# Two-layer block kernel: the order in which two mixers load projection chunks and modulation slots

## Chip, cores and metric

One core of one Trainium2 chip (trn2). The metric is the device time of one execution in microseconds, the median of three runs. Everything is float32 in memory.

## What is computed

The reference runs two blocks of two layers each over 256 tokens of width 1024. Only the first block's mixers matter here. Cut to that:

```python
cond = silu(c)
for layer in range(2):
    mod = dot(cond, ada_w[layer]) + ada_b[layer]          # 1024 -> 6144
    sh1, sc1, g1, sh2, sc2, g2 = split(mod, 6)
    u = x * (1 + sc1) + sh1
    proj = u @ w_in[layer]                                # 1024 -> 3088: six chunks of 512 and 16 "low" columns
    ...                                                   # short convolution, gated linear attention, w_out
    x = layernorm(ALPHA * x + (1 + g1) * mix)
    u = x * (1 + sc2) + sh2
    ...                                                   # feed-forward
```

The first third of the modulation (sh1, sc1) is wanted before u can be formed. The other two thirds are wanted only after the mixer, so the kernel computes them between the pieces of the input projection.

## The kernel before

The program is a list of stages (`stages()`), which every engine walks in the same order; the engines meet only at semaphores. The stage touched is "gla", which occurs twice, once per layer of the first block (the first and the second mixer). It starts with a stretch that computes `proj` and the other two thirds of `mod`:

- **Chunks.** C0 to C5 are each 1024 x 512 of `w_in`, 2 MiB. Matmuls are made from rounded halves: ACT rounds a quarter of a chunk into `l_hi` (`linear` in the scalar block, L1409 to L1426), DVE takes the remainder into `l_lo` (`linear_rest`, L1835), and TensorE multiplies hi by hi, hi by lo and lo by hi (`linear` in the tensor block, L741), 48 matmuls of 512 columns in each chunk. `l_hi` and `l_lo` have two buffers each, so a quarter is split while the one before it is multiplied. A filled chunk is copied by DVE into `proj` (L2160).
- **Slots.** A0 to A7 are each 256 x 2048 of `ada_w`, 2 MiB. `ada_slot` (L1068) multiplies one with `cond`, 16 small matmuls. It waits for both halves of its load. Slots A0 to A3 make modulation group 1, A4 to A7 group 2. When a group is complete ACT gathers it into `ada_rows` (`gather_rows`, L1428), TensorE spreads the rows over all partitions (`ada_spread_rows`, L1079) and DVE adds the bias (`add_rows`, L1842).
- **Low.** The last 16 columns of `w_in`, a load of 64 KB, multiplied after all chunks and slots (L1134). Everything of the gated attention follows it.

All 15 loads go through the two buffers `wide[0]` and `wide[1]` in turn: load w lies in buffer w % 2 (`RW = 2`). SP issues them in a fixed order, each as two halves of 1 MiB, and waits before each half until the buffer is free again (`fill`, L507 to L521, `wait_slot`, L498). A buffer that held a chunk is free for a first half when the remainder of its second quarter has been taken, and for the second half after the fourth; a buffer that held a slot is free for both when TensorE has used the slot. SP waits in order: a load that can't be issued holds up all behind it.

The order is written out by hand in three constants at the head of the file. `GLA_CHUNK_AT[c]` is the place of chunk c among the 15 loads, `GLA_ADA_AT[c]` are the places of the slots that TensorE uses behind chunk c, and low is at place 14:

```python
GLA_CHUNK_AT = (0, 2, 4, 7, 9, 11)
GLA_ADA_AT = ((1,), (3,), (5, 6), (8,), (10,), (12, 13))
```

So the order before is C0 A0 C1 A1 C2 A2 A3 C3 A4 C4 A5 C5 A6 A7 low. Group 1 is complete behind C2; its rows are spread in two parts, behind C3 and C4 (`ada_between`), and added by DVE one chunk later (`add_between`). ACT gathers group 1 after the second quarter of C3 (L1616).

Of the kernel before, what the change touches and what calls it, by code (L numbers as in the profile page):

```python
# [75 lines left out]

ADA_SLOTS = 4
ADA_COLS = 2048
GLA_CHUNK_AT = (0, 2, 4, 7, 9, 11)
GLA_ADA_AT = ((1,), (3,), (5, 6), (8,), (10,), (12, 13))  # L80
GLA_LOW_AT = 14


# [106 lines left out]
def build(nc, I, out):  # L190
# [29 lines left out]
    with ExitStack() as ctx:  # L220
# [8 lines left out]
        A = ctx.enter_context(nc.psum_tensor("A", [P, 4, 512], F32))  # L229
# [414 lines left out]
        def _(pe):  # L644
# [434 lines left out]
            def ada_spread_rows(group, banks, js=range(4)):  # L1079

                pe.wait_ge(ada_rows_ready, group + 1)
                for j in js:
                    if len(banks) == 4:
                        pe.wait_ge(ada_read, 4 * group)
                    elif group or j >= 2:
                        pe.wait_ge(ada_read, 4 * group + j - 1)
                    mm(banks[j % len(banks)], ones[32 * j:32 * j + 1, :], ada_rows[32 * j:32 * j + 1, :], True, True) \
                        .then_inc(ada_spread, 1)

            second_half = None  # L1090
            for index, (kind, arg, n, before) in enumerate(steps):
# [26 lines left out]
                elif kind == "gla":  # L1118
                    pe.wait_ge(t_evac, n.tg)

                    def ada_between(c):

                        for i, at in enumerate(GLA_ADA_AT[c]):
                            s = sum(map(len, GLA_ADA_AT[:c])) + i
                            group = 3 * arg + 1 + s // ADA_SLOTS
                            if s == 0 and n.free:
                                pe.wait_ge(acc_free, n.free)
                            ada_slot(n.w + at, group, s % ADA_SLOTS, A[:, 2 + s // ADA_SLOTS, :])
                        if c in (3, 4):
                            ada_spread_rows(3 * arg + 1, (A[:, 0, :], A[:, 1, :]), range(2 * c - 6, 2 * c - 4))  # L1130

                    linear(n, 6, uhv, ulv, 2, open_banks(n), linear_bank, g_done, True, between=ada_between)

# [232 lines left out]
        def _(act):  # L1366
# [222 lines left out]
            for index, (kind, arg, n, before) in enumerate(steps):  # L1589
                if kind == "start":  # L1590
                    act.wait_ge(s_c, 16)
                    nc.scalar.activation(condT, cT, ACT.Silu).then_inc(cond_ready, 1)
                elif kind == "ada":
                    gather_rows(3 * arg, G[:, 0, :])
                elif kind in ("trs8", "trs16"):
                    next_kind, m = split_early(index)
                    if next_kind == "ffn":
                        for q in range(4):
                            dense_rounder(m)(0, 0, q)
                    elif next_kind:  # L1600
                        linear(m, range(2))
                    groups = 4 if kind == "trs16" else 2
                    dst = (yh if kind == "trs16" else uh)[:, :].rearrange("p (k s) -> p k s", k=4 * groups)
                    for i in range(T * groups):
                        t, j = divmod(i, groups)
                        act.wait_ge(t_done, n.tg + i + 1)
                        nc.scalar.activation(dst[:, 4 * j:4 * j + 4, t * P:(t + 1) * P],
                                             TB[:, (n.tg + i) % 2, :].rearrange("p (k s) -> p k s", k=4), ACT.Copy) \
                            .then_inc(act_ready, 1)
                elif kind in ("out1", "out2"):  # L1610
                    linear(n, range(2, 8 if kind == "out1" else 16), acc_done, lambda c: n.acc + c + 1)
                elif kind == "tr8":
                    for j in range(4):
                        evac(n.tg + j, uT[:, 2 * j:2 * j + 2, :])
                elif kind == "gla":
                    linear(n, range(2, 14), g_done, lambda c: n.g + 2 * c + 2, slots=GLA_CHUNK_AT)  # L1616
                    gather_rows(3 * arg + 1, A[:, 2, :])
                    linear(n, range(14, 24), g_done, lambda c: n.g + 2 * c + 2, slots=GLA_CHUNK_AT)
                    gather_rows(3 * arg + 2, A[:, 3, :])
                    evac(n.tg, glowT[0:RANK, :], S, RANK)  # L1620
                    for t in range(T):
                        log_gate(n.g + 12 + t, lsg[:, t, :], KW)

                    evac(n.tg + 1, small[:, 52:60], 8, P, ACT.Exp)
                    act.wait_ge(dve_ready, n.dve + 3)
                    for t in range(T):
                        g = n.g + 16 + t
                        act.wait_ge(g_done, g + 1)
                        nc.scalar.activation(e3[:, t, 0:2 * KW], G[:, g % 2, 0:2 * KW], ACT.Exp)
                        nc.scalar.activation(e3[:, t, 2 * KW:3 * KW], G[:, g % 2, 0:KW], ACT.Exp, scale=-1.0) \  # L1630
                            .then_inc(act_ready, 1)
                    evac(n.tg + 2, gqT)
                    evac(n.tg + 3, gkT)
                    for t in range(T):
                        act.wait_ge(g_read, n.g + 16)
                        nc.scalar.activation(proj[:, t, C_H:C_H + VW], proj[:, t, C_G:C_G + VW], ACT.Silu) \
                            .then_inc(act_ready, 1)
                    for t in range(T):
                        g = n.g + 20 + t
                        act.wait_ge(g_done, g + 1)  # L1640
                        for h in range(HEADS):
                            sum_squares(g, t, h, DV, hbuf[:, t * VW + h * DV:t * VW + (h + 1) * DV], h == HEADS - 1)
                elif kind == "ffn":
                    run_dense(n)
                elif kind == "moe":
                    act.wait_ge(dve_ready, n.dve)
                    full = act.value_load(crowded[0:1, 0:1], min_val=0, max_val=1)
                    with act.If(full == 0):
                        with act.Fori(0, EXPERTS // 2) as i:
                            run_packed(n, i)  # L1650
                        act.drain().then_inc(act_ready, 3 * NU * EXPERTS - ACT_PAIR * (EXPERTS // 2))
                    with act.Else():
                        with act.Fori(0, EXPERTS // 2) as i:
                            run(n, PAIR, straight, i * PAIR, None)
                elif kind == "router":
                    act.wait_ge(dve_ready, n.dve + 1)
                    nc.scalar.activation(e2, gap, ACT.Exp).then_inc(act_ready, 1)
                elif kind == "kvdown":
                    for t in range(T):
                        act.wait_ge(g_done, n.g + t + 1)  # L1660
                        sum_squares(n.g + t, t, 0, KVLORA, sg[:, t * KVLORA:(t + 1) * KVLORA], True)
                    evac(n.tg, ckvT)
                    evac(n.tg + 1, krT, S)
                elif kind == "fox":
                    linear(n, range(2, 24), g_done, lambda c: n.g + 2 * c + 2)
                    for t in range(T):
                        log_gate(n.g + 12 + t, flt[:, t, :], FOX_H)
                    evac(n.tg, ncT[0:FOX_H, :], S, FOX_H, ACT.Copy, -1.0)
                    attention(n.tg + 1, 0)
                elif kind == "mla":  # L1670
                    for t in range(T):
                        act.wait_ge(g_done, n.g + t + 1)
                        sum_squares(n.g + t, t, 0, QLORA, hbuf[:, t * QLORA:(t + 1) * QLORA], True)
                    evac(n.tg, cqT[:, 0:2, :])
                    evac(n.tg + 1, cqT[:, 2, :], S)
                    for j in range(4):
                        evac(n.tg + 2 + j, qrT[:, 2 * j:2 * j + 2, :])
                    attention(n.tg + 6, GROUPS)
                elif kind == "ple":
                    linear(n, range(2, 8), g_done, lambda c: n.g + 2 * c + 2)  # L1680
                    evac(n.tg, pT)
                    for t in range(T):
                        act.wait_ge(g_read, n.g + 3 + t)
                        nc.scalar.activation(gt[:, t, :], gt[:, t, :], ACT.Sigmoid).then_inc(act_ready, 1)
# [73 lines left out]
        def _(dve):  # L1758
# [382 lines left out]
            for index, (kind, arg, n, before) in enumerate(steps):  # L2141
# [12 lines left out]
                elif kind == "gla":  # L2154

                    def add_between(c):
                        if c in (4, 5):
                            add_rows(arg, 1, (A[:, 0, :], A[:, 1, :]), range(2 * c - 8, 2 * c - 6))

                    linear(n, 6, lambda c, b: V.tensor_copy(proj[:, b, c * 512:(c + 1) * 512], linear_bank(c, b)),  # L2160
                           GLA_CHUNK_AT, add_between)
# [247 lines left out]
```

## Time and profile before

| | us |
|---|---|
| median of three runs | 2968.67 (2967.88 to 2969.22) |
| the profiled execution, its own time | 2973.35 |
| its span, first to last instruction | 2971.6 |
| first mixer: start of its C0, of its low projection | 57.15, 152.28 |
| second mixer: the same | 476.14, 572.55 |

The profile is of one execution. "PE" is TensorE's matmuls, "DVE" VectorE, "ACT" ScalarE, "SP" the engine whose queue issues the loads. Ends of matmuls are modelled, so durations of TensorE's work are best taken from start to start. Times are microseconds from the start of the span.

### The profile page before, as it was taken

The numbers are of one execution on the slowest core, as the hardware profiler recorded it, in microseconds if no ns is written. First come the engines' busy times: TensorE is split into PE (matmuls) and PEld (weight loads), VectorE is DVE, ScalarE is ACT, GpSimd is POOL, SyncE is SP. The second block draws the span as 40 slices with busy tenths as digits, with TensorE's granted clock in tenths as the row PEclk, the third lists the DMA queues.
The fourth block names the chain that finished last, engine by engine and source line by source line (L and its number), as shares of the span: only waits on it lengthen the run. The fifth ranks groups of instructions, "written<-read, shape, count | busy, mean of one in ns | idle before, by whom it ended". The sixth has DMA issues, their size and how long they took to land.

```text
span 2971.6 us, 33909 instructions
## 1 busy us (share of the span) xinstructions
PE 2598.4 (87%) x11836; PEld 2023.3 (68%) x11836; DVE 1714.6 (58%) x2044; ACT 1274.9 (43%) x1714; POOL 68.2 (2%) x88
## 2 busy tenths in 40 slices
PE   4978997767998998998999798988996998898996
PEld 2646874446776776776776686887874786687884
DVE  2446454455886886886787645535554554455545
ACT  1233432324665665665666333343431442043441
POOL 1000000000000000000000000000001000000001
PEclk7989998887999999999999899989998999999998
DMA  7816548724996996997899453406543643325551
GB/s 294 310 59 222 172 158 308 254 71 137 324 327 234 318 328 228 329 327 268 297 327 311 151 202 133 136 36 212 173 159 98 207 170 108 133 69 186 188 180 53
DMA packets 397402, 608.89 MB, mean 205 GB/s; under 512 B 14112, under 2 KB 317248, under 8 KB 390592
## 3 DMA queue, kind: packets, MB, share of 16 engines
q1 hardware_dynamic: 389648, 583.32, 57.3%
q0 software_dynamic: 6288, 22.55, 2.2%
q8 instruction: 87, 1.43, 0.2%
q10 hardware_dynamic: 1312, 1.05, 0.1%
q14 instruction: 67, 0.55, 0.1%
HBM read 605.83 MB, written 1.05 MB: 204 GB/s over the span
## 4 chain that ended last, share of the span: by engine, by line
PE 60%; DVE 17%; issue 12%; ACT 5%; DMA 4%; POOL 1%; ACTq 0%; DVEq 0%; SPq 0%
PE G L663 34%; PE A L663 18%; DVE w_lo L1876 9%; PE TB L663 4%; ACT w_hi L1463 4%; PE TB L685 2%; DMA wide<-in_moe_w_up 1%; PE TB L1036 1%; DVE hidden L1927 1%; DMA wide<-in_w_in 1%; DMA wide<-in_ada_w 1%; PE TB L935 1%; DVE small L2094 1%; DMA small<-in_c 1%; DVE x_tok L2106 1%
## 5 line engine op out<-in xcount | busy, mean ns | idle before, releaser
L1876 DVE TENSOR_TENSOR w_lo<-wide,w_hi 128x1024 fp32r<-128x1024 f32 x572 | 675.0, 1221 | 69.6 <-ACT w_hi L1463 65.3
L663 PE MATMUL G<-w_hi,u_hi 128*128 128x512 f32 x1584 | 646.6, 408 | 15.7 <-DVE u_lo L1901 6.4
L663 PE MATMUL G<-w_hi,u_lo 128*128 128x512 f32 x1584 | 621.9, 393 | 0.0
L663 PE MATMUL G<-w_lo,u_hi 128*128 128x512 f32 x1584 | 621.8, 393 | 0.0
L1463 ACT ACTIVATE w_hi<-wide 128x1024 fp32r<-128x1024 f32 x572 | 578.1, 1052 | 38.6 <-PE G L663 12.4
L663 PEld LDWEIGHTS G<-w_hi,u_hi 128*128 128x128 f32 x1584 | 299.8, 189 | 106.1 <-DVE w_lo L1876 34.9
L663 PEld LDWEIGHTS G<-w_hi,u_lo 128*128 128x128 f32 x1584 | 299.4, 189 | 66.0
L1876 DVE TENSOR_TENSOR w_lo<-down,w_hi 128x1024 fp32r<-128x1024 f32 x286 | 337.2, 1220 | 11.1 <-ACT w_hi L1463 10.4
L663 PEld LDWEIGHTS G<-w_lo,u_hi 128*128 128x128 f32 x1584 | 300.3, 190 | 57.9 <-issue 1.9
L663 PE MATMUL A<-w_hi,hidden_hi 128*128 128x512 f32 x792 | 317.3, 401 | 10.7 <-DVE w_lo L1876 10.7
L663 PE MATMUL A<-w_hi,hidden_lo 128*128 128x512 f32 x792 | 315.2, 398 | 0.0
L663 PE MATMUL A<-w_lo,hidden_hi 128*128 128x512 f32 x792 | 314.9, 398 | 0.0
L1838 DVE TENSOR_TENSOR l_lo<-wide,l_hi 128x1024 fp32r<-128x1024 f32 x128 | 155.9, 1224 | 237.3 <-ACT l_hi L1425 224.4
L1463 ACT ACTIVATE w_hi<-down 128x1024 fp32r<-128x1024 f32 x286 | 285.9, 1049 | 6.7 <-PE G L663 6.7
L1425 ACT ACTIVATE l_hi<-wide 128x1024 fp32r<-128x1024 f32 x128 | 134.3, 1059 | 294.7 <-PE G L663 101.7
L2001 DVE TENSOR_TENSOR hidden_lo<-TB,hidden_hi 128x512 fp32r<-128x512 f32 x50 | 34.6, 692 | 270.1 <-ACT hidden_hi L1551 270.1
L663 PEld LDWEIGHTS A<-w_hi,hidden_hi 128*128 128x128 f32 x792 | 149.7, 189 | 46.1 <-DVE w_lo L1876 11.7
L663 PEld LDWEIGHTS A<-w_hi,hidden_lo 128*128 128x128 f32 x792 | 150.2, 190 | 37.0
L663 PEld LDWEIGHTS A<-w_lo,hidden_hi 128*128 128x128 f32 x792 | 150.1, 190 | 35.6
L1551 ACT ACTIVATE hidden_hi<-TB 128x512 fp32r<-128x512 f32 x50 | 30.0, 600 | 261.1 <-PE TB L935 261.1
L1505 ACT ACTIVATE hidden_hi<-TB 128x256 fp32r<-128x256 f32 x88 | 33.9, 385 | 229.2 <-PE TB L1036 229.2
L1547 ACT ACTIVATE silu_gate<-G 128x256 f32<-128x256 f32 x110 | 42.5, 386 | 208.5 <-PE G L663 208.5
(252 smaller groups left out, 2919.1 us busy)
## 6 DMA issues: line engine op xcount, KB each, us to landing
wide<-in_moe_w_gate SPq DMA_DIRECT2D x88, 1024.0 KB, 5.5
wide<-in_moe_w_up SPq DMA_DIRECT2D x88, 1024.0 KB, 8.5
down<-in_moe_w_down SPq DMA_DIRECT2D x88, 1024.0 KB, 9.4
wide<-in_ffn_w_in SPq DMA_DIRECT2D x88, 1024.0 KB, 7.6
wide<-in_ada_w SPq DMA_DIRECT2D x48, 1024.0 KB, 7.1
down<-in_ffn_w_out SPq DMA_DIRECT2D x44, 1024.0 KB, 8.5
wide<-in_w_in SPq DMA_DIRECT2D x24, 1024.0 KB, 6.9
wide<-in_fox_w_in SPq DMA_DIRECT2D x12, 1024.0 KB, 5.2
```

Of the source, the lines that this page charges most:

```text
L663: return nc.tensor.matmul(o, lhsT, rhs, start=start, stop=stop, skip_group_check=True)
L685: last = nc.tensor.transpose(TB[:, tg % 2, b * P:(b + 1) * P], block_in, ident)
L935: last = nc.tensor.transpose(TB[:, (n.tg + j) % 2, f * S + t * P:f * S + (t + 1) * P], hid[:, 0, t, tok(f)], ident)
L1036: last = nc.tensor.transpose(TB[:, (n.tg + c) % 2, tok(f)], hid[:, 0, 0, tok(f)], ident)
L1425: nc.scalar.activation(ring[p % depth], wide[w % RW][:, q * 1024:(q + 1) * 1024], ACT.Copy) \
L1463: nc.scalar.activation(to[:, :], raw, ACT.Copy).then_inc(hi_ready, 1)
L1505: nc.scalar.activation(hth[:, 0:2 * P], TB[:, (n.tg + c) % 2, 0:2 * P], ACT.Copy).then_inc(act_ready, 1)
L1547: nc.scalar.activation(sgt[:, t, :], G[:, t, 0:FU], ACT.Silu).then_inc(act_ready, 1)
L1551: nc.scalar.activation(hth[:, :], TB[:, (n.tg + j) % 2, :], ACT.Copy).then_inc(act_ready, 1)
L1838: V.tensor_tensor(l_lo[at][:, :], wide[(n.w + slots[c]) % RW][:, q * 1024:(q + 1) * 1024], l_hi[at][:, :].bitcast(F32), ALU.subtract).then ...
L1876: V.tensor_tensor(w_lo[to][:, :], raw, w_hi[to][:, :].bitcast(F32), ALU.subtract).then_inc(lo_ready, 1)
L2001: V.tensor_tensor(htl[:, :], TB[:, (n.tg + j) % 2, :], hth[:, :].bitcast(F32), ALU.subtract) \
```

## The change

The three orders are rewritten: chunks go in pairs, then slots in pairs. The rows of group 1 are spread behind C4 and C5 in place of C3 and C4 and added by DVE one chunk later than before, and ACT gathers them after the second quarter of C4. The new order is C0 C1 A0 A1 C2 C3 A2 A3 C4 C5 A4 A5 A6 A7 low.

```diff
-GLA_CHUNK_AT = (0, 2, 4, 7, 9, 11)
-GLA_ADA_AT = ((1,), (3,), (5, 6), (8,), (10,), (12, 13))
+GLA_CHUNK_AT = (0, 1, 4, 5, 8, 9)
+GLA_ADA_AT = ((), (2, 3), (), (6, 7), (), (10, 11, 12, 13))
 GLA_LOW_AT = 14
...
-                        if c in (3, 4):
-                            ada_spread_rows(3 * arg + 1, (A[:, 0, :], A[:, 1, :]), range(2 * c - 6, 2 * c - 4))
+                        if c in (4, 5):
+                            ada_spread_rows(3 * arg + 1, (A[:, 0, :], A[:, 1, :]), range(2 * c - 8, 2 * c - 6))
...
-                    linear(n, range(2, 14), g_done, lambda c: n.g + 2 * c + 2, slots=GLA_CHUNK_AT)
+                    linear(n, range(2, 18), g_done, lambda c: n.g + 2 * c + 2, slots=GLA_CHUNK_AT)
                     gather_rows(3 * arg + 1, A[:, 2, :])
-                    linear(n, range(14, 24), g_done, lambda c: n.g + 2 * c + 2, slots=GLA_CHUNK_AT)
+                    linear(n, range(18, 24), g_done, lambda c: n.g + 2 * c + 2, slots=GLA_CHUNK_AT)
                     gather_rows(3 * arg + 2, A[:, 3, :])
...
-                        if c in (4, 5):
-                            add_rows(arg, 1, (A[:, 0, :], A[:, 1, :]), range(2 * c - 8, 2 * c - 6))
+                        if c in (5, 6):
+                            add_rows(arg, 1, (A[:, 0, :], A[:, 1, :]), range(2 * c - 10, 2 * c - 8))
```

## Rows read from the trace of the kernel before

**Rows 1.** The page, busy time, share of the span, instructions, by engine.

```profile
PE 2598.4 (87%) x11836; PEld 2023.3 (68%) x11836; DVE 1714.6 (58%) x2044; ACT 1274.9 (43%) x1714; POOL 68.2 (2%) x88
```

**Rows 2.** The page, the chain that ended last, shares by engine.

```profile
PE 60%; DVE 17%; issue 12%; ACT 5%; DMA 4%; POOL 1%; ACTq 0%; DVEq 0%; SPq 0%
```

**Rows 3.** TensorE's waits, 57 to 153 us: total, times, longest us.

```profile
PE TB L663 <- DVE l_lo L1838: 5.6, 1, 5.6
```

**Rows 4.** Timeline of TensorE, first mixer: start, us, instruction, idle before and releaser.

```profile
70.67 1.92 PE L663 MATMUL A<-wide,small 128*32 128x512 f32 x16
72.52 0.50 PE L663 MATMUL TB<-l_hi,u_hi 128*128 128x512 f32 x1
...
83.73 1.92 PE L663 MATMUL A<-wide,small 128*32 128x512 f32 x16
...
106.19 0.80 PE L663 MATMUL TB<-l_hi,u_hi 128*128 128x512 f32 x1 [5.60 <-DVE l_lo L1838]
...
119.14 1.92 PE L663 MATMUL A<-wide,small 128*32 128x512 f32 x16
...
122.05 0.50 PE L663 MATMUL G<-l_hi,u_hi 128*128 128x512 f32 x1
...
152.28 0.59 PE L663 MATMUL TB<-u_hi,wide 128*16 128x256 f32 x2 [1.14 <-DMA wide<-in_w_in]
```

**Rows 5.** Timeline of SP's queue, loads issued: start, us.

```profile
72.65 0.34 SPq L517 DMA_DIRECT2D wide<-in_ada_w  x1
73.03 0.43 SPq L519 DMA_DIRECT2D wide<-in_ada_w  x1
73.51 0.43 SPq L517 DMA_DIRECT2D wide<-in_w_in  x1
80.66 0.38 SPq L519 DMA_DIRECT2D wide<-in_w_in  x1
...
98.72 0.38 SPq L517 DMA_DIRECT2D wide<-in_w_in  x1
...
518.16 0.38 SPq L517 DMA_DIRECT2D wide<-in_w_in  x1
```

**Rows 6.** Landings: of 98.72; of 80.66; of 72.65 and 73.03; with 73.51.

```profile
DMA to landing us min/median/max: 5.1/5.1/5.1
...
DMA to landing us min/median/max: 5.2/5.2/5.2
...
DMA to landing us min/median/max: 5.0/6.1/7.2
...
DMA to landing us min/median/max: 5.0/7.2/9.3
```

**Rows 7.** Timeline of DVE, first mixer.

```profile
69.20 1.23 DVE L1838 TENSOR_TENSOR l_lo<-wide,l_hi 128x1024 fp32r<-128x1024 f32 x1 [1.57 <-ACT l_hi L1425]
...
104.91 2.36 DVE L1838 TENSOR_TENSOR l_lo<-wide,l_hi 128x1024 fp32r<-128x1024 f32 x2 [11.21 <-ACT l_hi L1425]
```

**Rows 8.** Stretches: length, busy us by engine, granted clock, DMA share, GB/s.

```profile
70.67:106.19 35.52, 29.92 (x161) 19.45 (x161) 12.17 (x13) 9.70 (x10) 0.00 (x0) 0.96 0.85 317
106.19:119.14 12.95, 12.95 (x48) 10.19 (x49) 5.96 (x6) 3.30 (x4) 0.00 (x0) 0.85 0.72 266
```

**Rows 9.** Timeline of TensorE, second mixer.

```profile
490.05 1.92 PE L663 MATMUL A<-wide,small 128*32 128x512 f32 x16
...
526.75 0.79 PE L663 MATMUL TB<-l_hi,u_hi 128*128 128x512 f32 x1 [6.65 <-DVE l_lo L1838]
...
539.33 1.92 PE L663 MATMUL A<-wide,small 128*32 128x512 f32 x16
...
572.55 0.59 PE L663 MATMUL TB<-u_hi,wide 128*16 128x256 f32 x2 [0.96 <-issue]
```

**Rows 10.** Timeline of DVE, behind the first mixer's low projection.

```profile
160.50 2.48 DVE L1848 TENSOR_TENSOR arena<-A,arena 128x512 f32<-128x512 f32 x4 [12.36 <-PE A L663]
```

**Rows 11.** Timeline of TensorE, the third slot ahead of the first mixer.

```profile
30.08 3.64 PE L663 MATMUL G<-wide,small 128*32 128x512 f32 x16 [6.56 <-DMA wide<-in_ada_w]
```

## The prediction

> **What bounds the kernel now.** I read the page first: busy times and the chain that ended last. TensorE is busy 87% of the span [rows 1], and 60% of the chain is TensorE with DMA at 4% [rows 2]. A load matters only where TensorE runs dry for it, so the question is where it does so inside the two mixers. The list of who waited for whom, taken over the first mixer's projection stretch (57.15 to 152.28 us), is led by 5.6 us put down to DVE's l_lo, the last link between a load and its product [rows 3]. The timeline of TensorE gives the places [rows 4]: 1.14 us ahead of the low projection at 152.28, and the 5.60 us ahead of the fourth chunk (C3), at 106.19, right behind the one place where two modulation slots follow each other. That chunk lay in a buffer freed only at the end of the first of the two slots: SP issued it at 98.72 [rows 5], its first half landed 5.1 us after the issue [rows 6], ACT rounded it, DVE took its remainder from 104.91 [rows 7], TensorE began at 106.19. So one rule governs: **a chunk behind a modulation slot in its own buffer comes 106.19 - 98.72 = 7.47 us after that slot is used.** Everywhere else one slot lies between chunk c and chunk c+1, the other buffer holds that slot, and the next chunk's halves load while chunk c is still multiplied. In that stretch DMA is 85% busy at 317 GB/s [rows 8]. The second mixer repeats it: 6.65 us ahead of C3 [rows 9].
>
> Unit prices, all start to start in rows 4: a chunk 83.73 - 72.52 = 11.21 us; a modulation slot 72.52 - 70.67 = 1.85; a slot with a spread of two rows behind it 122.05 - 119.14 = 2.91, the spread thus 1.06; the chunk behind the stall 119.14 - 106.19 = 12.95, so 1.74 more. In rows 9 the last is 539.33 - 526.75 = 12.58.
>
> **The change, step by step.** No instruction is added or removed: the same 6 chunks, 8 slots and 15 loads, hence the same bytes. What moves is the order, on TensorE, on SP (each load waits in order for its own buffer) and in two places on ACT and DVE. New order: C0 C1 A0 A1 C2 C3 A2 A3 C4 C5 A4 A5 A6 A7 low, even places in buffer 0, odd in buffer 1. I follow the first mixer from the end of C0, 70.67, which stays (C1 now loads in the place of A0, before C0 begins).
>
> 1. C1 follows C0 directly: 70.7 to 81.9. Its first weights must be split; in rows 7 the piece begun by DVE at 69.20 took 1.23 us and ended 70.43, so this is covered.
> 2. A0 runs to 83.7 (its buffer was free halfway through C0). A1's second half waits for C1's last split, which came 80.66 - 72.52 = 8.14 us into the chunk [rows 4, 5]: 78.8, plus 5.2 to land [rows 6] gives 84.0. A1 ends 85.9; 0.3 us lost.
> 3. C2 shares buffer 0 with A0. SP issues it at 83.75 and TensorE has it at 83.75 + 7.47 = 91.2. **Idle 5.3 us**, where before there was none. The chunk behind is the 12.95 us kind: to 104.2. C3, issued at 85.9 behind it, is in time: to 115.4.
> 4. The same again: A2 to 117.2, A3 to 119.4, C4 ready at 117.3 + 7.47 = 124.7. **Idle 5.3 us**, then 12.95 to 137.7. This stall stands for the old one at C3. Spread 1.06, C5 to 149.9.
> 5. The tail. Before, one slot stood before C5 and the last two were in or nearly so. Now four stand behind it, and two of them have no buffer until A4 and A5 are used. A4 ends 151.8. A5's second half is issued 138.7 + 8.14 = 146.9 and is in at 152.0; A5 ends 153.8. A6 is issued at 151.8: rows 6 give 5.0 us for the first half and 7.2 for the second issued 0.38 later, so it is in at 159.4. **Idle 5.6 us.** A7, issued 153.8, queues behind it; three halves in a row landed at 77.65, 80.2 and 82.8 [rows 5, 6], 2.6 us each, so A7 is in at 164.6. **Idle 3.3 us**, after A6 ended 161.3. A7 to 166.4, the spread that used to stand before C5 to 167.5. The low projection's small load, issued 161.3, lands before that, so its old 1.14 us wait is gone.
>
> Low starts at 167.5 instead of 152.28: **15.2 us later.** As a sum from 70.67: work is 5 x 11.21 + 8 x 1.85 + 2 x 1.06 = 73.0 both times; before 5.60 + 1.14 idle and 1.74 slow chunk make 81.5 (81.61 read); now about 20 idle and 3.5 slow. The added moves on the other engines are free: ACT's gather of the second group and two of DVE's adds (four took 2.48 us [rows 10], so 1.2 for the two, and the gather, of the same 512 columns, 0.6) now fall under the low projection, which with its spread filled 152.28 to 160.50, some 7 us without the spread. I cost them at nothing because that covers them; without it they would be 2 us per mixer. Nothing takes the delay up later: DVE had stood idle 12.36 us for TensorE before those adds [rows 10]. The loads of w_out behind are the next stage's.
>
> Second mixer, from 490.05 to 572.55 [rows 9], 82.5 us: the same list with 12.58 for 12.95 (twice) gives 96.1, so **13.6 us**. Here the issue at 518.16 took 8.59 us to the product instead of 7.47 [rows 5, 9]; the ends for each of the four boundary stalls are 7.47 and 8.59 and I keep 7.47, three of the neighbouring landings being 5.0 to 5.2.
>
> **TensorE's clock in the tail** is shown by no row. What the rows have: after an idle stretch of 6.56 us a modulation slot took 3.64 us instead of 1.92 [rows 11], and after 5.60 us a chunk lost 1.74. A6's loss hides in the wait for A7. For A7 and low I bound it by 0 (warm again) and 3.4 (two such losses), and take 1.0 per mixer, nearer to the lower end since A6 and A7 stand close together. On this the Trainium skill, "TensorE: Matmul & The Clock Gate", on oscillation, says that kernels with idle stretches for DMA between short bursts run their matmuls at half rate after every gap and pay half the throttled time. The trace agrees in kind: over the chunk behind the stall the granted clock was 0.85, against 0.96 over the stretch before it [rows 8]. And by that rule the tail's low projection could stay at 1.2 GHz; that is rival C.
>
> **Sum:** 15.2 + 13.6 + 2.0 = 30.8 us. The profiled execution has a span of 2971.6 and a time of 2973.35; with the change 3002.4 and 3004.15. The median of the runs is 2968.67, 4.7 below the profiled one, so I forecast **2999.5 us**. For the load latency, the skill's "DMA: Bandwidth & Descriptors", on the anatomy of one DMA, fits 2.0 us plus bytes over 436 GB/s, which is an estimated 4.4 us for a half of 1 MiB; rows 6 have 5.0 to 5.2, and the measurement decides. By that fit each of the six waits would be 0.6 to 0.8 shorter and the answer 2995.
>
> **Rivals.** (A) *Faster.* The pairing takes away the double slot between C2 and C3 and puts nothing in its place: the ring would cover C2 and C4 because the buffer opens early. Worth 5.60 + 1.74 + 6.65 + 1.4 = 15.4 us, 2953. It decides at one point: C2 must be issued by 85.9 - 7.47 = 78.4, over 5 us before A0 ends. Only if buffer 0 were given back before A0 was used could that be; SP's wait on the slot says no. (B) *No change.* The stage is bound by the rate of the loads (85% busy), the bytes are the same, and order doesn't matter: 2969. Against it: 28 MiB at 2.6 us per MiB are 73 us in 81.6, so there is slack for TensorE to set the pace, and the new order leaves DMA with nothing to do in C1's and C3's second halves. (C) *Clock.* The tail's gaps keep TensorE at 1.2 GHz through low, 7 us of work: 7 instead of 1 per mixer, 3011. For it: two gaps with only 1.85 us of work between them. Against: low is unbroken, and the chunk behind 5.60 us of idle lost only 1.74, so there the full rate came back within 4 us. (D) *Smaller.* The tail's wait is taken up elsewhere and only the boundaries count: (0.3 + 5.3 + 0.2 + 5.3 + 1.74 - 5.6) = 7.2 per mixer, 2983.
>
> **How the numbers follow.** Forecast, with its own bounds: 0.80. Rival C 0.08, D 0.04, A 0.04, B 0.04. Lower bound of the forecast: no loss in the tail (-2), and the chunks behind a stall at the plain 11.21 for the one new stall in each mixer (-3), and landings 0.6 shorter on six waits (-4): 2990. Upper: 8.59 on four boundary stalls (+4.5) and 3.4 instead of 1 in each tail (+5): 3009. That holds 8 in 10, so the range stays there. A measurement of this kernel can tell about 0.2% (6 us) from no change: faster 0.04, same 0.04, slower 0.92.
>
> **What would show it.** In the profile after: the waits of TensorE should have two stalls of 5 to 6 us per mixer, ahead of C2 and of C4, put down to DVE's l_lo, and none ahead of C3; two waits for DMA wide<-in_ada_w near the end, 5.6 and 3.3 us; SP issuing C2 right after A0 is used; low 15 us later than 152.28, the second mixer's low some 29 later than 572.55; everything between and behind shifted unchanged. The forecast is wrong if C2 begins within 2 us of A1's end, if A6 and A7 run back to back, or if the stretch between low and the next stage shrinks by what the tail grew.

## The result, and the profile after

The changed kernel takes 3001.21 us (median of 5 runs, 2999.35 to 3003.94) against 2969.22 us (5 runs) for the kernel before: a ratio of 1.0108, 95% interval 1.0094 to 1.0122, or 32.0 us more. Forecast was 2999.5. The profiled execution took 3002.36 us with a span of 3000.6, 29.0 us more than the span before.

The page answers to rows 1 and 2 almost without a change: TensorE is busy 7 us longer, with the same 11836 matmuls.

```profile
PE 2605.3 (87%) x11836; PEld 2025.7 (68%) x11836; DVE 1714.3 (57%) x2044; ACT 1274.0 (42%) x1714; POOL 68.1 (2%) x88
```

The waits of TensorE tell more. First mixer, 57 to 170 us, the view of rows 3:

```profile
PE G L663 <- DVE l_lo L1838: 13.7, 2, 7.2
PE A L663 <- DMA wide<-in_ada_w: 8.2, 3, 6.7
PE G L663 <- DVE u_lo L2057: 1.4, 1, 1.4
```

Second mixer, 480 to 610 us:

```profile
PE G L663 <- DVE l_lo L1838: 11.1, 2, 5.7
PE A L663 <- DMA wide<-in_ada_w: 7.1, 3, 5.7
```

Each mixer has two waits for a chunk in place of one, and 8.2 and 7.1 us of waits for slots, where the kernel before had none and 0.3. The timeline of TensorE, first mixer (as rows 4), has their places:

```profile
81.25 1.92 PE L663 MATMUL A<-wide,small 128*32 128x512 f32 x16
...
91.81 0.79 PE L663 MATMUL G<-l_hi,u_hi 128*128 128x512 f32 x1 [6.57 <-DVE l_lo L1838]
...
115.80 1.92 PE L663 MATMUL A<-wide,small 128*32 128x512 f32 x16
117.90 1.92 PE L663 MATMUL A<-wide,small 128*32 128x512 f32 x16 [0.18 <-DMA wide<-in_ada_w]
...
126.99 0.79 PE L663 MATMUL G<-l_hi,u_hi 128*128 128x512 f32 x1 [7.17 <-DVE l_lo L1838]
...
139.51 1.13 PE L663 MATMUL A<-ada_rows,con 1*128 1x512 f32 x4
...
162.31 3.64 PE L663 MATMUL A<-wide,small 128*32 128x512 f32 x16 [6.68 <-DMA wide<-in_ada_w]
...
167.25 3.64 PE L663 MATMUL A<-wide,small 128*32 128x512 f32 x16 [1.30 <-DMA wide<-in_ada_w]
...
171.89 0.61 PE L663 MATMUL TB<-u_hi,wide 128*16 128x256 f32 x2
...
178.90 1.14 PE L663 MATMUL A<-ada_rows,con 1*128 1x512 f32 x8
```

C2 at 91.81 and C4 at 126.99 are the two boundaries, A6 at 162.31 and A7 at 167.25 the tail, 171.89 the start of low, which has no wait of its own any more. The second mixer (as rows 9):

```profile
530.37 0.80 PE L663 MATMUL G<-l_hi,u_hi 128*128 128x512 f32 x1 [5.46 <-DVE l_lo L1838]
...
564.82 0.80 PE L663 MATMUL G<-l_hi,u_hi 128*128 128x512 f32 x1 [5.68 <-DVE l_lo L1838]
...
600.19 3.64 PE L663 MATMUL A<-wide,small 128*32 128x512 f32 x16 [5.65 <-DMA wide<-in_ada_w]
605.15 1.92 PE L663 MATMUL A<-wide,small 128*32 128x512 f32 x16 [1.32 <-DMA wide<-in_ada_w]
...
608.06 0.61 PE L663 MATMUL TB<-u_hi,wide 128*16 128x256 f32 x2
```

SP's queue shows when the chunks behind were issued (as rows 5): C2 right behind A0 (81.25 + 1.92), C4 behind A2.

```profile
83.23 0.38 SPq L517 DMA_DIRECT2D wide<-in_w_in  x1
...
117.78 0.38 SPq L517 DMA_DIRECT2D wide<-in_w_in  x1
...
522.99 0.38 SPq L517 DMA_DIRECT2D wide<-in_w_in  x1
...
557.10 0.38 SPq L517 DMA_DIRECT2D wide<-in_w_in  x1
```

From issue to product these are 8.58, 9.21, 7.38 and 7.72 us, where the kernel before had 7.47 and 8.59. Counted from C0 to the start of low, the stretch grew from 95.13 to 115.05 us in the first mixer (56.84 to 171.89) and from 96.41 to 111.89 in the second (496.17 to 608.06): 19.9 and 15.5 us, together 35.4. Behind the second mixer the offset between the two profiled executions shrank again to 29.0; the repeat of the kernel before, below, is about that.

### The profile page after: what moved, and what is told of

Read it like the earlier page. It is cut to its first block, busy times and chain, and to the rows that moved or that the text cites. A ratio compares the mean times of both kernels' runs of the same rounds, so it can differ in the third digit from the quotient of the medians.

```text
span 3000.6 us, 33909 instructions
## 1 busy us (share of the span) xinstructions
PE 2605.3 (87%) x11836; PEld 2025.7 (68%) x11836; DVE 1714.3 (57%) x2044; ACT 1274.0 (42%) x1714; POOL 68.1 (2%) x88
## 3 DMA queue, kind: packets, MB, share of 16 engines
q10 hardware_dynamic: 1312, 1.05, 0.1%
HBM read 605.83 MB, written 1.05 MB: 202 GB/s over the span
## 4 chain that ended last, share of the span: by engine, by line
PE 60%; DVE 18%; issue 12%; ACT 5%; DMA 4%; POOL 1%; ACTq 0%; DVEq 0%; SPq 0%
PE G L663 34%; PE A L663 17%; DVE w_lo L1876 10%; PE TB L663 4%; ACT w_hi L1463 4%; PE TB L685 2%; DMA wide<-in_ada_w 1%; PE TB L1036 1%; DVE hidden L1927 1%; DMA wide<-in_w_in 1%; PE TB L935 1%; DVE small L2094 1%; DMA small<-in_c 1%; DVE x_tok L2106 1%; DVE u_lo L2057 1%
## 5 line engine op out<-in xcount | busy, mean ns | idle before, releaser
L1876 DVE TENSOR_TENSOR w_lo<-down,w_hi 128x1024 fp32r<-128x1024 f32 x286 | 337.2, 1220 | 11.1 <-ACT w_hi L1463 10.5
```

Of the source, the lines that this page charges most:

```text
L1876: V.tensor_tensor(w_lo[to][:, :], raw, w_hi[to][:, :].bitcast(F32), ALU.subtract).then_inc(lo_ready, 1)
```

## Experiments

The theory is that of the forecast: a load can be issued only when TensorE has used the slot in its buffer, and is exposed wherever no more than one slot's work stands between; behind the wait some work runs at the lower clock. Four kernels were run first, two that split the change and two repeats.

**One pair alone.** The kernel before with C1 ahead of A0, and nothing else.

```diff
-GLA_CHUNK_AT = (0, 2, 4, 7, 9, 11)
-GLA_ADA_AT = ((1,), (3,), (5, 6), (8,), (10,), (12, 13))
+GLA_CHUNK_AT = (0, 1, 4, 7, 9, 11)
+GLA_ADA_AT = ((), (2, 3), (5, 6), (8,), (10,), (12, 13))
```

> The kernel before with one thing of the change: C1 comes ahead of A0, so that the order is C0 C1 A0 A1 C2 A2 A3 C3 and from there as before. Theory (a chunk that lies in the buffer of the slot just used comes about 7.5 us after that slot): a new stall of 5.3 to 6.6 us ahead of C2 in each mixer, the old one ahead of C3 stays, C2 loses 1.3 to 1.7 us to the half clock, tail unchanged: 7 to 8 us per mixer, 2983 to 2985 us in all, half of what the change cost. Rival (pairing chunks is free, all of the cost lies in the four slots at the end): 2969 us and no stall ahead of C2.

Measured: 2986.01 us, ratio 1.0058 (1.0041 to 1.0075), or 17.8 us more. Its waits of TensorE in the first mixer:

```profile
PE G L663 <- DVE l_lo L1838: 6.8, 1, 6.8
PE TB L663 <- DVE l_lo L1838: 5.8, 1, 5.8
```

The new one (G, an even chunk: C2) stands beside the old one (TB, an odd chunk: C3), in the second mixer as 5.8 beside 7.3. Pairing is not free; one boundary costs about 9 us per mixer. The interval of the ratio allows 6 to 11, so that this is more than the 7 to 8 expected is not shown. From issue to product the loads took 8.74 us (C2) and 7.69 (C3) in the first mixer, 7.64 and 9.29 in the second.

**The tail alone.** From the changed kernel, with a slot between all chunks up to C4:

```diff
-GLA_CHUNK_AT = (0, 1, 4, 5, 8, 9)
-GLA_ADA_AT = ((), (2, 3), (), (6, 7), (), (10, 11, 12, 13))
+GLA_CHUNK_AT = (0, 2, 4, 6, 8, 9)
+GLA_ADA_AT = ((1,), (3,), (5,), (7,), (), (10, 11, 12, 13))
```

> The other part alone: order C0 A0 C1 A1 C2 A2 C3 A3 C4 C5 A4 A5 A6 A7 low. Every chunk but C5 has a slot between it and the one before, so no stall ahead of C2, C3, C4; the four slots stand at the end as in the changed kernel. Theory: the old stall at C3 goes (minus 5.6 and 1.7 us; 6.65 and 1.4 in the second mixer), the tail costs two waits of 5.6 to 6.7 and 1.3 to 3.3 us plus slow slots, about 10 us per mixer against the tail before: plus 2 to 3 us per mixer, 2973 to 2975 us. Rival (the tail's waits are taken up behind the low projection, only the boundaries count): 7.5 us less per mixer, 2954 us. Rival (the clock stays at the lower level through low and beyond): 2985 us.

Measured: 2973.48 us (12 runs), ratio 1.0019 (1.0008 to 1.0030). The first mixer's waits before low:

```profile
PE A L663 <- DMA wide<-in_ada_w: 7.4, 3, 5.1
PE G L663 <- DVE u_lo L2057: 1.4, 1, 1.4
```

No wait for a chunk is left in the first mixer (the second keeps 0.70 us ahead of C3), and the slots' waits are there: 5.05 for A6, 1.71 for A7 and 0.62 for A5. The old stall gone and the tail added nearly cancel, as expected; both rivals (2954, 2985) are out. With the stall at 7.3 and 8.0 us per mixer this puts the two tails at 5.3 + 15.3 = 20.6 us. The changed kernel less one_pair, which has as many boundary stalls but the tail of before, gives 32.0 - 17.8 = 14.2. The profile's own count for the changed kernel (waits for A6 and A7 and what the slots took over 1.92, less the 1.14 and 0.96 that went ahead of low) is 18.0, between the two. The ratios' intervals are several us wide, so 14 to 21 us for the two tails is all that these three can say.

**The changed kernel again.**

> The changed kernel once more, for a second look at the four boundary waits and the two tail waits of each mixer. Theory: the longer ones of the first mixer (6.6, 7.2 and 6.7 us, where 5.3 to 5.6 were forecast) are late landings that vary from execution to execution; then they come out differently, between 5.3 and 7.2. Rival: something in the first mixer makes its loads slower each time; then the same three stand within 0.3 us, and the second mixer's at 5.5 to 5.7 again.

Measured: one run, 3005.05 us. From issue to product the four chunks took 8.77, 8.97, 7.91 and 7.35 us; the wait for A6 in the first mixer was 6.6 and in the second 5.6. This settles neither side. The three long waits of the first mixer came again as 6.7, 6.8 and 6.6 us, the second of them 0.4 off, outside the rival's 0.3; the second mixer's came as 6.1, 5.4 and 5.6. Long waits are not bound to the first mixer either: one_pair has its longest in the second, and so have both executions of the kernel before.

**The kernel before again.**

> The kernel before once more. In the two profiled executions the offset between the kernels fell from 35 us behind the second mixer to 29 us at the end, most of it in the expert stage. Theory: this is the spread of single executions in stages that the change doesn't touch; then this execution stands 2 to 6 us earlier than the first one at the end of the expert stage. Rival: the changed order shifts something that makes the expert stage shorter by 6 us; then this execution keeps within 1 us of the first one all the way.

Measured: one run, 2965.32 us. Matmul for matmul it stands 0.9 us behind the first execution at the start of the first mixer and 1.5 behind at the second mixer's low, then 3.4 ahead of it at 1630 us, 4.8 at 2237 and 8.0 at the end. This is one kernel against itself, so offsets of some us in the stages behind are the spread of single executions. Between the two repeats the offset does the opposite: 34.2 us at the second mixer's low, 39.7 at the end. So the 6 us that the first pair of executions seemed to give back are not shown to be an effect of the change. The two mixers themselves, from C0 to low, repeat more closely: 191.5 and 191.6 us in the kernel before, 226.9 and 224.0 in the changed one.

**Idle matmuls in the waits.** In `ada_between` of the changed kernel, behind each slot:

```diff
+                            if s in (1, 3):
+                                for _ in range(22):
+                                    mm(A[:, 0, :], uhv[:, 0, tok(0)], uh[:, 0:512], True, True)
+                            if s in (5, 6):
+                                pe.wait_ge(g_read, n.g + 10)
+                                for _ in range(22 if s == 5 else 10):
+                                    mm(G[:, 0, :], uhv[:, 0, tok(0)], uh[:, 0:512], True, True)
```

> The changed kernel with idle matmuls in its waits: 22 of 512 columns behind A1 and A3 (into a bank not yet in use), 22 behind A5 and 10 behind A6, in each mixer; the results are overwritten and nothing else is changed. They take 5.0 us and 2.3 us, less than the waits. Theory: the waits for loads stay, but TensorE goes on at 2.4 GHz behind them: C2 and C4 take 11.2 us instead of 12.5 to 12.9, A6 1.9 instead of 3.6 (partly given back as a longer wait for A7), A7 1.9 in both mixers: 3 to 5 us less per mixer, 2992 to 2995 us. Rival (the chunk behind a stall is slower because its splits come late, not through the clock): no change, 3001 us.

Measured: 2991.48 us, ratio to before 1.0072 (1.0059 to 1.0084), so about 10 us under the changed kernel with 152 more matmuls, just better than the expected range. The timeline of its first mixer behind C3:

```profile
113.22 1.92 PE L663 MATMUL A<-wide,small 128*32 128x512 f32 x16
116.38 1.92 PE L663 MATMUL A<-wide,small 128*32 128x512 f32 x16 [1.23 <-DMA wide<-in_ada_w]
```

C2, first product at 91.08, and C3 together took 22.14 us up to 113.22, where the changed kernel needed 115.80 - 91.81 = 23.99 and two undisturbed chunks are 22.42 by rows 4. C4 of the second mixer shows it best, first in the changed kernel, then here (as rows 8; the granted clock is third from the end):

```profile
564.82:578.55 13.73, 13.73 (x48) 10.75 (x48) 5.95 (x6) 3.29 (x4) 0.00 (x0) 0.80 0.70 253
...
554.19:565.40 11.21, 11.21 (x49) 8.86 (x49) 5.95 (x6) 3.30 (x4) 0.00 (x0) 1.00 0.87 318
```

All four chunks behind a wait took 11.1 to 11.2 us at the full clock, against 12.5 to 13.7 at 0.79 to 0.88, and A6 and A7 took 1.92 each. The first halves still landed 5.1 to 6.3 us after their issue and no split got shorter, so the slower chunk is the clock's. Not all of the 10 us is: the four landings add up to 21.8 us here and to 23.3 and 23.5 in the two executions of the changed kernel. The clock's part there is thus an estimated 8 us or a little more (the kernel before has some of it too, at its C3).

**One slot between any two chunks.** From the changed kernel:

```diff
-GLA_CHUNK_AT = (0, 1, 4, 5, 8, 9)
-GLA_ADA_AT = ((), (2, 3), (), (6, 7), (), (10, 11, 12, 13))
+GLA_CHUNK_AT = (0, 2, 4, 6, 8, 10)
+GLA_ADA_AT = ((1,), (3,), (5,), (7,), (9,), (11, 12, 13))
```

> Order C0 A0 C1 A1 C2 A2 C3 A3 C4 A4 C5 A5 A6 A7 low: one slot between any two chunks, three at the end. Theory: no stall ahead of any chunk, and one wait in the tail, for A7, which gets its buffer only when A5 has been used: 5.6 us plus 0 to 1.7 for its clock; the 1.1 us ahead of low go. Against before minus 7.3 and plus 5 to 6 per mixer: 2965 to 2968 us, within 0.2 per cent of before, and 34 us under the changed kernel. Rival (one double slot costs less anywhere but ahead of a chunk): 2955 us.

Measured: 2966.99 us (12 runs), ratio 0.9991 (0.9980 to 1.0001): not to be told from before. In the first mixer 5.9 us of waits for slots remain, 4.6 of them ahead of A7. One wait for a chunk was not expected: 1.92 us ahead of C3 in the second mixer (1.1 and 1.2 at the same place in the two kernels that follow). Nor was what stands behind A7: TensorE's timeline there has

```profile
148.15 3.64 PE L663 MATMUL A<-wide,small 128*32 128x512 f32 x16 [4.62 <-DMA wide<-in_ada_w]
...
153.73 1.04 PE L663 MATMUL TB<-u_hi,wide 128*16 128x256 f32 x2
...
163.60 1.14 PE L663 MATMUL A<-ada_rows,con 1*128 1x512 f32 x8
```

Low took 9.87 us here (153.73 to 163.60), and 8.64 in the second mixer (576.05 to 584.69), instead of 7.0; its first pairs of matmuls stand 0.85 us apart, the later ones 0.43. The granted clock over the first mixer's low was 0.71. This is what rival C had described, in part and in another kernel. So a double slot moved to the end costs as much as one ahead of a chunk, its share of the clock included; the time came out in the expected range although that share, of 2.9 and 1.6 us in low, was not in the sum.

**Low ahead of the last slot.** As the one before, and the low projection moved into A7's wait:

```diff
-GLA_ADA_AT = ((1,), (3,), (5,), (7,), (9,), (11, 12, 13))
-GLA_LOW_AT = 14
+GLA_ADA_AT = ((1,), (3,), (5,), (7,), (9,), (11, 12))
+GLA_LAST_ADA_AT = 14
+GLA_LOW_AT = 13
...
                     fill(v[:, :, C_LOW:C_LOW + RANK], KD, RANK, (t_done, n.tg + 1))
+                    fill_ada(arg, 2, ADA_SLOTS - 1)
...
                     last.then_inc(t_done, 1)
+                    ada_slot(n.w + GLA_LAST_ADA_AT, 3 * arg + 2, ADA_SLOTS - 1, A[:, 3, :])
                     ada_spread_rows(3 * arg + 2, [A[:, j, :] for j in range(4)])
...
-                    gather_rows(3 * arg + 2, A[:, 3, :])
                     evac(n.tg, glowT[0:RANK, :], S, RANK)
+                    gather_rows(3 * arg + 2, A[:, 3, :])
```

> As all_single, but the low projection with its load stands ahead of A7, at place 13, and A7 at place 14; ACT evacuates low before it gathers the last rows. Theory: A7's load, issued when A6 has been used, lands under the 7 us of low, so that the tail has no wait for a load above 1 us; the gather and the spread behind A7 put 2 to 3 us between low and the first addition instead of 1.2. Against all_single minus 4 to 5 us per mixer: 2955 to 2959 us, faster than before by 0.3 to 0.5 per cent. Rival (what is hidden in the tail is lost again behind A7, since DVE waits for the spread): 2965 us.

Measured: 2951.96 us, ratio 0.9944 (0.9930 to 0.9958), 3 us better than the expected range. Its waits in the first mixer:

```profile
PE G L665 <- DVE arena L1781: 5.7, 1, 5.7
PE G L665 <- DVE u_lo L2060: 1.4, 1, 1.4
PE A L665 <- DMA wide<-in_ada_w: 1.3, 1, 1.3
PE A L665 <- ACT ada_rows L1436: 0.7, 1, 0.7
```

The load waits are down to 1.3 us (at most 1 was expected), the gather behind A7 costs 0.7, and the wait for DVE's gate step, 7.0 us in the kernel before, is now the largest. It is no shorter in effect: from the spread to the convolution's first matmul it is 9.88 us here (152.15 to 162.03) as in the kernel before (159.27 to 169.15), here first:

```profile
152.15 1.14 PE L665 MATMUL A<-ada_rows,con 1*128 1x512 f32 x8 [0.71 <-ACT ada_rows L1436]
...
162.03 11.63 PE L665 MATMUL G<-arena,con 128*128 128x512 f32 x24 [5.68 <-DVE arena L1781]
...
159.27 1.14 PE L663 MATMUL A<-ada_rows,con 1*128 1x512 f32 x8
...
169.15 11.93 PE L663 MATMUL G<-arena,con 128*128 128x512 f32 x24 [7.02 <-DVE arena L1778]
```

The gain over all_single, 15 us where 8 to 10 were expected, is larger because not only A7's wait went but what followed from it: in the first mixer A7 took 1.92 us for 3.64, and low 7.02 for 9.87.

**DVE's additions later.** The same, and `add_rows` of the last group moved:

```diff
-                    add_rows(arg, 2, [A[:, j, :] for j in range(4)])
-                    dve.wait_ge(ada_read, 4 * (3 * arg + 3))
                     dve.wait_ge(g_read, n.g + 12)
...
                         V.tensor_scalar(gk[:, t, :], lsg[:, t, :], 1.0 / 16.0, -1.0, ALU.mult, ALU.max) \
                             .then_inc(dve_ready, 1)
+                    add_rows(arg, 2, [A[:, j, :] for j in range(4)])
+                    dve.wait_ge(ada_read, 4 * (3 * arg + 3))
```

> The low_first order, and DVE's four additions of the last group (2.48 us) moved from ahead of the convolution to behind the two gate steps, where DVE then stands idle 4.4 us for TensorE. Theory: DVE sets the pace between low and the convolution's matmuls, so this takes about 2.5 to 4 us off each mixer: 2944 to 2947 us. Rival (those matmuls wait for the clock or for something else as well): 2950 to 2952 us.

Measured: 2947.19 us, ratio 0.9934 (0.9921 to 0.9948), the lowest median here, though the interval overlaps that of low_first: by the times alone the two can't be told apart. The profile can: from the spread to the convolution's first matmul it is 6.47 us in both mixers, 3.4 less than in low_first. DVE set the pace there, and still does:

```profile
PE G L665 <- DVE arena L1781: 3.6, 1, 3.6
PE G L665 <- DVE u_lo L2060: 1.4, 1, 1.4
```

**The other layer's weights.** This is about the term that came out too small. SP loads, in each mixer, the chunks and slots of the other layer:

```diff
-                    v = kview(I["w_in"][arg])
+                    v = kview(I["w_in"][1 - arg])
...
-                v = kview(I["ada_w"][l])[:, 2 * s:2 * s + 2, group * ADA_COLS:(group + 1) * ADA_COLS]
+                v = kview(I["ada_w"][l if group == 0 else 1 - l])[:, 2 * s:2 * s + 2, group * ADA_COLS:(group + 1) * ADA_COLS]
```

> The changed kernel, but each mixer loads the chunks and slots of the other layer, so that the output is another one; order, sizes and waits are the same. It is for the term that was sized too small: in the first mixer the loads behind an idle stretch took 8.6 to 9.2 us from issue to the first product, in the second 7.4 to 7.9, in both executions of the changed kernel. Theory (it is the place of the data in memory): the first mixer then shows 7.4 to 7.9 and the second 8.6 to 9.2. Rival (it is the place in the program): as before the swap.

Measured: one run, 3000.20 us; from issue to product 8.72, 7.95, 7.43 and 7.63 us. The second mixer did not become slower, so which layer's weights are loaded is not it. The first boundary stays at 8.6 to 8.8 in all three executions of this order, but the second went from 9.2 and 9.0 to 7.95, so the place in the program isn't the whole of it either.

The other executions show what a late load consists of. These are the stretches of the changed kernel from the issue of C2 and C4 to the landing of the first half, first mixer and then second (as rows 8; the last number is GB/s):

```profile
83.23:89.43 6.20, 1.92 (x16) 0.49 (x16) 0.00 (x0) 0.00 (x0) 0.00 (x0) 0.96 0.83 290
117.78:124.58 6.80, 1.92 (x16) 0.49 (x16) 0.00 (x0) 0.00 (x0) 0.00 (x0) 0.89 0.85 297
522.99:527.99 5.00, 1.92 (x16) 0.47 (x16) 0.00 (x0) 0.00 (x0) 0.00 (x0) 1.00 0.78 265
557.10:562.40 5.30, 1.92 (x16) 0.49 (x16) 0.00 (x0) 0.00 (x0) 0.00 (x0) 1.00 0.77 267
```

The late ones are not slower in GB/s. Length times rate gives 1.80, 2.02, 1.32 and 1.42 MB moved by the time the half of 1.05 MB was complete; nearly all of the rest belongs to the loads issued behind it. The same two numbers for every chunk that lay in the buffer of the slot just used, in each profiled execution:

| kernel | first mixer: us to landing, MB moved | second mixer |
|---|---|---|
| before | 5.1, 1.31 | 6.2, 1.74 |
| before again | 5.0, 1.31 | 6.0, 1.67 |
| one_pair, C2 and C3 | 6.3, 1.81; 5.3, 1.39 | 5.3, 1.39; 6.9, 2.01 |
| changed, C2 and C4 | 6.2, 1.80; 6.8, 2.02 | 5.0, 1.32; 5.3, 1.42 |
| changed again | 6.4, 1.83; 6.6, 1.90 | 5.5, 1.45; 5.0, 1.31 |
| other layer's weights | 6.3, 1.81; 5.6, 1.54 | 5.0, 1.30; 5.2, 1.34 |
| idle matmuls | 5.3, 1.42; 5.1, 1.37 | 6.3, 1.81; 5.1, 1.35 |

Time and bytes rise together in all 24: where a first half lands late, more of the loads behind it had been moved by then, in either mixer. What decides how much goes ahead stays open.

## Why the prediction was right

**The rule (a chunk comes so many us after the slot whose buffer it takes)** held at every one of the four boundaries, and in one_pair, at the places forecast; the time is not fixed, as the step had it. Where the step said 5.3 us of idle, the first mixer had 6.57 and 7.17 and the second 5.46 and 5.68. The term that was mis-sized most is the time from issue to product: I took 7.47, of the two rows there were, and kept 8.59 for the range. The four measured 7.38 to 9.21, their mean 8.22, near the upper row. The landings say it is the load and not the split. C2's first half, first mixer and second:

```profile
DMA to landing us min/median/max: 6.2/6.2/6.2
...
DMA to landing us min/median/max: 5.0/5.0/5.0
```

The fit in the Trainium skill, "DMA: Bandwidth & Descriptors", on the anatomy of one DMA, is given there for loads that GpSimd issues, while SP issues these. The estimate of 4.4 us worked out from it, which would have made the answer 2995, is further from the 5.0 to 6.8 measured than rows 6 were.

**The chunk behind a stall** was forecast to lose 1.74 us in the first mixer and 1.37 in the second. C2 and C4 lost 1.57 and 1.31 in the first (C2 taken with C3, over 22.42), but 2.33 and 2.52 in the second, where this and not the load is the larger miss: its two waits were only 0.5 us too long in sum.

**The tail** was right in sum and wrong in its parts. A6 waited 6.68 and 5.65 us (5.6 forecast), A7 1.30 and 1.32 (3.3 forecast). The forecast for A7 was too long because it let A6 run 1.85 us: I had noted that a slow A6 would hide in that wait, and it did. Stretches of the changed kernel (length, busy us by engine, granted clock third from the end), A6, A7 and low of the first mixer, then of the second:

```profile
162.31:165.95 3.64, 3.64 (x16) 0.65 (x16) 0.00 (x0) 0.00 (x0) 0.00 (x0) 0.50 0.84 353
167.25:170.82 3.57, 3.57 (x16) 0.65 (x17) 0.00 (x0) 0.00 (x0) 0.00 (x0) 0.50 0.17 16
171.89:178.90 7.01, 7.01 (x35) 3.02 (x33) 1.29 (x2) 0.60 (x1) 0.00 (x0) 1.00 0.84 301
...
600.19:603.83 3.64, 3.64 (x16) 0.65 (x16) 0.00 (x0) 0.00 (x0) 0.00 (x0) 0.50 1.01 428
605.15:607.00 1.85, 1.85 (x16) 0.46 (x17) 0.00 (x0) 0.00 (x0) 0.00 (x0) 1.00 0.33 31
608.06:615.07 7.01, 7.01 (x35) 3.02 (x33) 1.29 (x2) 0.60 (x1) 0.00 (x0) 1.00 0.87 302
```

A6 ran at half clock (1.2 GHz) in both mixers, A7 in the first alone, low at the full 2.4 GHz in both and in the 7.0 us it took before. The term for the clock was 1.0 us per mixer behind A6; it measured 1.7 and 0, and 0 twice in the repeat. Rival C, in which low pays as well, did not occur in any execution of this order; all_single shows that it can.

The Trainium skill, "TensorE: Matmul & The Clock Gate", on oscillation, says of a kernel with short bursts between waits for DMA that each burst starts at half rate. The trace agrees for the start of C2 and C4 and for the whole of A6, all behind 5.5 to 7.2 us without work, and for one of two A7s, behind 1.3. It goes no further: over the whole of C2 and C4 the granted clock was 0.79 to 0.88, and by the time low began the full rate was back.

**Nothing takes it up later** held: rival D fell with tail_only, which was 5 us slower than before and not 15 faster, and in the changed kernel the wait for DVE's gate step is 6.5 and 7.0 us where it was 7.0. **Rival A** asked that C2's load be issued before A0 was used; SP issued it at 83.23, behind A0. **Rival B** (same bytes, same time): the bytes are the same, and yet the time grew by 32 us while the rate over the span fell from 204 to 202 GB/s.

In the profiled execution the two mixers grew by 35.4 us where 30.8 were forecast. The terms, over both mixers:

| term | forecast, us | measured, us |
|---|---|---|
| waits ahead of C2 and C4 | 21.2 | 24.9 |
| chunks slower behind them | 6.2 | 7.7 |
| waits for A6 and A7 | 17.8 | 15.0 |
| slower A6 and A7, beyond the forecast waits | 2.0 | 5.2 |
| short waits for A1 and A3 | 1.0 | 0.4 |

C0 was 0.4 us shorter, which makes up the rest. The boundaries came out 5 us dearer than forecast. In the tail the two errors of 3 us are one, seen from two sides: A6 took 1.7 us longer and left as much less of A7's wait. That the rest, 1.7 us at one of two A7s against the 2.0 set down, came so near is luck: the forecast had picked it between two bounds, and in the repeat it was 0. Repeats of both kernels grew by 32.4 us, the execution with the other layer's weights by 32.3 and the median by 32.0, so the forecast was 1 to 2 us low in the sum and not 5.

## What to carry to other kernels

In a ring of two buffers, write down for every load which use frees its buffer and how much work stands between that use and the load's own; where that is less than issue-to-product time (here 7.4 to 9.3 us, against 1.85 for a slot and 11.2 for a chunk) the engine stands idle by the difference. Spread short consumers singly between long ones, and put one too many where independent work can stand in its wait, as the low projection here: the first alone gained nothing (0.9991), with the second the kernel was 0.6% faster. Price such a wait by the rows with the longer latency, and add one stretch at the lower clock for each.

## What I had not expected of the hardware

- Loads of the same size and shape took 5.0 to 6.9 us from issue to landing, in either mixer. The late ones did not move at a lower rate: 1.7 to 2.0 MB had been moved when the half of 1.05 MB was complete, against 1.3 to 1.5 MB for the early ones. So more of the loads issued behind had gone ahead of its end; why more at one time than at another is open.
- Filling the waits with useless matmuls made the changed kernel about 10 us faster, of which an estimated 8 or more are the clock's.
- Where a single modulation slot stood between a wait of 4.5 us and low, low began at the lower clock; where two stood there, with 1.3 us between them, it did not, even when the second of them ran at 1.2 GHz.
